# An early load of the query weights' second chunk, and a first unit that gathers partly into the weight ring

## The reference

```python
def peer_ffn(h, wq, sub_keys, u, v):          # wq: 1024 x 2048, u and v: 16384 x 1024
    ...
        q = (xt @ wq).astype(f32).reshape(PEER_TOKEN_BLOCK, PEER_HEADS, 2, PEER_DKEY // 2)
        s = jnp.einsum('thcd,hckd->thck', q, sub_keys.astype(f32))
        top_s, top_i = lax.top_k(s, PEER_TOPK)
        cand = top_s[:, :, 0, :, None] + top_s[:, :, 1, None, :]
        best_s, best_c = lax.top_k(cand.reshape(PEER_TOKEN_BLOCK, PEER_HEADS, PEER_TOPK * PEER_TOPK), PEER_TOPK)
        ...
        expert = i1 * PEER_NKEYS + i2
        w = jax.nn.softmax(best_s, axis=-1)
        act = jax.nn.gelu(jnp.einsum('thkd,td->thk', u[expert].astype(f32), xt.astype(f32)))
        return jnp.einsum('thk,thkd->td', w * act, v[expert].astype(f32))
```

## Time and profile before

| | |
|---|---|
| median of 3 runs | 1526.77 us (1526.72 to 1533.27) |
| the profiled execution: its own time | 1526.57 us |
| its span in the profile | 1524.7 us |
| TensorE busy | 1360.8 us, 89% |
| VectorE busy | 1039.5 us, 68% |
| ScalarE busy | 589.9 us, 39% |
| GpSimd busy | 516.3 us, 34% |
| moved by the DMA engines | 413.69 MB, 271 GB/s over the span |

### The profile page before, as it was taken

How to read it: one execution, slowest core, us unless ns; L and a number is a source line. 1 busy time by engine, 2 the same in 40 slices (tenths; PEclk the granted TensorE clock), 3 DMA queues, 4 the chain that set the end, 5 groups by cost and what they waited for, 6 DMA issues and landing times.

```text
span 1524.7 us, 16289 instructions
## 1 busy us (share of the span) xinstructions
PE 1360.8 (89%) x5950; PEld 900.7 (59%) x5950; DVE 1039.5 (68%) x1860; ACT 589.9 (39%) x908; POOL 516.3 (34%) x554
## 2 busy tenths in 40 slices
PE   9999998777877777777777899999999999999998
PEld 7965677222322222222222368789888897798887
DVE  4655589656666675756557676778897575688963
ACT  4553322212221111111122266855655454555642
POOL 5000046777777777777777600000000000000000
PEclk9999999999999999999999999999999999999999
DMA  9523189999999999999999954326564454356552
GB/s 295 213 78 138 63 334 404 409 409 409 409 409 409 409 409 409 410 409 410 409 409 410 390 180 168 123 97 209 172 216 166 160 201 166 103 174 206 181 195 81
DMA packets 162751, 413.69 MB, mean 271 GB/s; under 512 B 11249, under 2 KB 57579, under 8 KB 162544
## 3 DMA queue, kind: packets, MB, share of 16 engines
q0 software_dynamic: 75664, 272.63, 45.4%
q1 hardware_dynamic: 86832, 139.94, 26.5%
q10 hardware_dynamic: 176, 0.07, 0.0%
HBM read 411.56 MB, written 1.05 MB: 271 GB/s over the span
## 4 chain that ended last, share of the span: by engine, by line
PE 54%; DMA 21%; POOL 8%; DVE 8%; issue 5%; ACT 4%; ACTq 0%; DVEq 0%; POOLq 0%
PE ps L1516 10%; DMA arena<-in_peer_u,routes 9%; PE ps L1536 8%; PE ps L854 7%; PE ps L1352 7%; PE ps L1524 5%; DMA ring<-in_peer_v,routes 5%; POOL arena L3299 4%; DMA aTm<-in_peer_v,routes 3%; DMA proj<-in_peer_v,routes 3%; DVE arena L2826 2%; POOL ring L3310 2%; PE ps L1507 2%; PE ps L1211 1%; PE ps L1239 1%
## 5 line engine op out<-in xcount | busy, mean ns | idle before, releaser
L2826 DVE SCALAR_TENSOR_TENSOR arena<-arena,ps 128x1024 f32<-128x1024 f32 x256 | 312.0, 1219 | 212.8 <-DMA arena<-in_peer_u,routes 211.8
L3299 POOL DMA_INDIRECT arena<-in_peer_u,routes x256 | 249.2, 974 | 113.8 <-DVE arena L2826 50.6
L2054 ACT ACTIVATE state<-cst,gatew 128x128 f32<-128x128 f32 x236 | 88.1, 397 | 307.2 <-PE ps L1352 297.3
L2389 DVE TENSOR_TENSOR w_lo<-ring,w_hi 128x2048 fp32r<-128x2048 f32 x66 | 150.9, 2289 | 71.9 <-ACT w_hi L2201 71.9
L1352 PE MATMUL ps<-ring,state 128*128 128x512 f32 x308 | 150.0, 610 | 45.8 <-ACT state L2054 29.0
L1516 PE MATMUL ps<-x_both,w_hi 128*128 128x512 f32 x640 | 160.3, 392 | 0.0
L2201 ACT ACTIVATE w_hi<-ring 128x2048 fp32r<-128x2048 f32 x66 | 126.0, 1912 | 68.3 <-PE ps L1536 49.9
L1352 PEld LDWEIGHTS ps<-ring,state 128*128 128x128 f32 x308 | 52.5, 189 | 140.5 <-issue 71.5
L1516 PEld LDWEIGHTS ps<-x_both,w_hi 128*128 128x128 f32 x640 | 115.1, 189 | 20.6
L1352 PE MATMUL ps<-proj,state 128*128 128x512 f32 x160 | 78.1, 610 | 24.9 <-ACT state L2054 15.1
L1352 PE MATMUL ps<-wX,state 128*128 128x512 f32 x156 | 76.2, 610 | 23.8 <-ACT state L2054 15.1
(11 more groups left out here) (547 smaller groups left out, 2515.2 us busy)
## 6 DMA issues: line engine op xcount, KB each, us to landing
ring<-in_ffn_w_up SPq DMA_DIRECT2D x22, 2048.0 KB, 8.6
ring<-in_ffn_w_down SPq DMA_DIRECT2D x10, 2048.0 KB, 7.6
ring<-in_even_w_in SPq DMA_DIRECT2D x7, 2048.0 KB, 7.7
ring<-in_w_in SPq DMA_DIRECT2D x6, 2048.0 KB, 10.4
ring<-in_odd_w_in SPq DMA_DIRECT2D x6, 2048.0 KB, 7.7
ring<-in_peer_wq SPq DMA_DIRECT2D x3, 2048.0 KB, 9.4
ring<-in_w_out SPq DMA_DIRECT2D x2, 2048.0 KB, 7.8
arena<-in_peer_u,routes POOLq DMA_INDIRECT x256, 16.0
```

The costliest lines, as they stand in the source:

```text
L2054: do(diags[n % DIAGS], ident, ACT.Copy, scale=gatew[:, u * UROWS + b:u * UROWS + b + 1]).then_inc(diag_ready, 1)
L2389: v.tensor_tensor(w_lo[j % 2][:], w, w_hi[j % 2][:].bitcast(F32), ALU.subtract).then_inc(lo_ready, 1)
L2826: v.scalar_tensor_tensor(row, row, 1.0, token_tile(u // PAIR_UNITS), ALU.mult, ALU.mult, accum_out=dots[:, b:b + 1]).then_inc(u_used, 1)
L3299: pool.indirect_dma_start(arena[:, b % GATHER_SLOTS, :], None, a["peer_u"][0], route_of(u, b))\
```

## The change

The second query chunk, `IN_ARENA`, leaves the ring. It is loaded into the first four places of `arena` as soon as the mixer's recurrent part has read them (`cl_o_done`), ahead of the early pieces of the third chunk, with `consts_in` as its semaphore. Every later chunk of the ring moves up by one place in the order: the fourth query chunk goes where the second was, and follows the first chunk of `w_out`; `ple_gate_w` follows the second chunk of `w_out` and the first query chunk.

Since four places of `arena` hold weights at first, the rows of `peer_u` get new addresses (`u_row`). Places 0 to 3 of the eight are now `arena` 4 to 7. Places 4 to 7 are, for the first 24 rows (`FIRST_ROWS_END`), quarters of the ring place that the second chunk of `w_out` had, and later `arena` 0 to 3. Three waits come with it: the fifth gather waits for the second chunk of `w_out` to be used, the twenty-ninth for the second query chunk, and the load of the first `ple_gate_w` chunk into that ring place for 24 used rows.

```diff
-BESIDE_RING = (CHUNK_AT["peer_wq"] + 2, CHUNK_AT["ple_proj"])
+IN_ARENA = CHUNK_AT["peer_wq"] + 1
+BESIDE_RING = (IN_ARENA, CHUNK_AT["peer_wq"] + 2, CHUNK_AT["ple_proj"])
...
+FIRST_PLACES, FIRST_ROWS_END = RING_PLACE[CHUNK_AT["w_out"] + 1][0], 24
+assert FIRST_PLACES == RING_PLACE[CHUNK_AT["ple_gate_w"]][0]
...
+        def u_row(n):
+
+            at = n % GATHER_SLOTS
+            if at < 4:
+                return arena[:, 4 + at, :]
+            return ring[:, FIRST_PLACES, 1024 * (at - 4):1024 * (at - 3)] if n < FIRST_ROWS_END else arena[:, at - 4, :]
+
         def loaded(i):
 
+            if i == IN_ARENA:
+                return consts_in, 32
             if i in BESIDE_RING:
                 return beside_loaded, 16 * N_BESIDE
...
             n = chunk_width(name, c)
+            if i == IN_ARENA:
+                return grid(block(0, 4), KD, n)
             return slot(i)[:, 0:KD * n].rearrange("p (k n) -> p k n", k=KD)
...
             for i, (name, c) in enumerate(CHUNKS):
-                if i in BESIDE_RING:
+                if i in BESIDE_RING and i != IN_ARENA:
                     continue
...
                     sp.wait_ge(cl_o_done, 2)
+                    sp.dma_start(product_slot(IN_ARENA), weights["peer_wq"][:, :, 512:1024]).then_inc(consts_in, 16)
                     sp.dma_start(grid(query_rows[0], 2, 512), early[:, 0:2, :]).then_inc(beside_loaded, 16)
...
                     sp.dma_start(mixed[:].rearrange("p a (k n) -> p (a k) n", k=2), early[:, 4:8, :]).then_inc(beside_loaded, 16)
+                    continue
                 at, _, _, free = RING_PLACE[i]
                 if free:
                     sp.wait_ge(chunk_done, free)
+                if (name, c) == ("ple_gate_w", 0):
+                    sp.wait_ge(u_used, FIRST_ROWS_END)
...
-                    row = arena[:, b % GATHER_SLOTS, :]
+                    row = u_row(b)
                     dve.wait_ge(u_landed[b % GATHER_SLOTS], 16 * (b // GATHER_SLOTS + 1))
...
-                pool.indirect_dma_start(arena[:, b % GATHER_SLOTS, :], None, a["peer_u"][0], route_of(u, b))\
+                if n == 4:
+                    pool.wait_ge(chunk_done, CHUNK_AT["w_out"] + 2)
+                if n == FIRST_ROWS_END + 4:
+                    pool.wait_ge(chunk_done, IN_ARENA + 1)
+                pool.indirect_dma_start(u_row(n), None, a["peer_u"][0], route_of(u, b))\
                     .then_inc(u_landed[b % GATHER_SLOTS], 16)
```

## The result

The changed kernel takes 1531.22 us (median of 22 runs, 1530.2 to 1532.59), the kernel before 1526.96 us (22 runs, median): a ratio of 1.0026, 95% interval 1.0020 to 1.0032. It is 4.3 us slower; the forecast was 3.8 us. The profiled execution has a span of 1529.1 us, 4.4 more than before.

A forecast was written before the change was run, and what follows sets the result against it. Expert-row gathers at 409 GB/s bound the kernel, VectorE pacing their ramp (201 to 253 us). At 253 us, 3.74 MB gate weights left less 2.17 MB more gathers moved, over 0.409, gives +3.8 us: 1530.4 us; range 1523.5 to 1534.0.

The forecast's parts named there:

- VectorE starts 1.6 us sooner, routes at about 251.3 us: Before the gather plateau: VectorE begins choosing unit 1's experts 1.6 us sooner; routes at 251.3, not 252.92 us.
- Gate loads at 250.0 us: End of the ramp: both ple_gate_w chunks, 4.19 MB, wait for 24 used rows and are issued at 250.0 us.
- Gathers moved by 253 us, 16.25 MB: Ramp, 201 to 253 us: 31 expert rows landed, 16.25 MB, 2.17 MB more than before.
- The estimate of 3.2 us: Ramp: alternative landing time per gathered row, against 4.0 us used; nearly half the thirty-second row in, sum below 0.6 us less.
- 0.45 MB of the gate loads by 253 us: End of the ramp: 0.45 MB of ple_gate_w moved by 253.0 us, 3.74 MB left.
- 308 GB/s between 220 and 250 us: Ramp: gathers alone, paced by VectorE at 1.70 us per 0.524 MB row, move near 308 GB/s in place of 400.
- The plateau starts full: Expert gathers from 253 us on: all bytes left were priced at 0.409 MB/us, with no slower start.
- The first rival: Expert stage from 204 us: DMA engines already full, so 2.1 MB taken out save 5.1 us, 1521.4 us; chance 0.13.
- the start that sets the end: Gather plateau paced by GpSimd's issue, so it ends 1.6 us sooner with the routes: 1525.0 us; chance 0.07.
- The large loss: Ramp: no more than 27 rows in by 253 us, all 4.19 MB gate weights added: 10.2 us, 1536.8 us; chance 0.12.
- The price at nothing of the new addresses and GpSimd's waits: First 32 gathers: their new row places and the added waits of the fifth and twenty-ninth cost nothing.

The follow-up runs named there:

- halved products: VectorE multiplies only 512 of 1024 columns of the first 32 rows: 1524.63 us in the changed kernel, 1526.89 us in the kernel before.
- two extra loads: Changed kernel loading its second gate chunk twice: extra load at about 219 us, 1531.64 and 1531.37 us; both loads after 96 used rows, 1537.03 us.

## Why the prediction was right

The time was right, and so was the mechanism; some terms were off and one was missing, and that they nearly cancel is luck. Term by term:

- *VectorE starts 1.6 us sooner, routes at about 251.3 us*: 1.65 us, and 251.04. TensorE begins on the second query chunk without a wait:

```profile
200.56 7.31 PE L1287 MATMUL ps<-xT,arena 128*128 128x128 f32 x64
```

  But not every gather from the tenth on is issued 1.6 us sooner: the tenth goes out 0.05 us sooner and the eleventh 1.0, at GpSimd's own pace, and only from the thirteenth on it is 1.6. The halved products show that VectorE's instructions are what paces the gathers there.
- *Gate loads at 250.0 us*: 249.99. Their wait alone makes the kernel before 5.8 us slower; that they go out late is the cause of the loss, shown from both kernels.
- *Gathers moved by 253 us, 16.25 MB*: 16.25 MB, but the way there was not clean. I took 4.0 us for a gather to land. None in the ramp did; this is the landing row of the gathers into `arena` up to 253 us in the changed kernel:

```profile
DMA to landing us min/median/max: 5.1/6.0/10.0
```

  So the thirty-first row, issued at 248.44 us, had not landed whole by 253. Bytes of rows under way are moved too, which the step left out; that the two errors cancel to the second decimal is luck. The estimate of 3.2 us that I worked out from the Trainium skill (DMA: Bandwidth & Descriptors, Anatomy of one DMA) lies still further from the 5.1 us at least that were measured; and by that fit 0.7 us of bytes, 0.3 MB of the thirty-second row, would have been in, more than the half that the prediction gave it.
- *0.45 MB of the gate loads by 253 us*: 0.20. With it the sum would have been 1.8 MB and 4.4 us.
- *308 GB/s between 220 and 250 us*: 367, 327 and 311 in the three windows. The rate was reached only at the end, because the first rows, issued at GpSimd's own pace, left a queue that lasted until about 224 us (404 GB/s from 222 to 224 us, 361 in the next two).
- *The plateau starts full*: not so. In the changed kernel 250 to 260 us run at 342 GB/s. The gate loads behind it fill some of this, and without them it is worse by 1.6 us. This term was missing. From 253 to 262 us the changed kernel moves 383 GB/s, the kernel before 407: 0.21 MB, 0.5 us. The tail gave as much back, since from 860 to 875 us the changed kernel moves 409 and the kernel before 395; the prediction had neither.
- The first rival (bytes of a full stage, 5.1 us less) is refuted by the two extra loads; the start that sets the end by the result itself (routes sooner, last row later) and by the halved products. The large loss didn't come either: its condition was 14.1 MB of rows or less by 253 us, and 16.25 were in. The price at nothing of the new addresses and GpSimd's waits stands: with them in place, one load in another order brings the whole loss back.

## What to carry to other kernels

A stage whose transfer engines are full may still have free time in it: ask who would fill it if one of the streams were gone. Here a transfer was nearly free where a compute engine paced the others (0.2 to 0.4 us for 2.1 MB), and cost its bytes divided by the rate or a little more where the engines set the pace (5.3 to 5.8 us); so an early load helps only if what moves up behind it is not pushed out of the free time into the full one. In an in-order queue, look at what the new wait holds back: here a load whose place was free 31 us earlier stood behind one whose place was not.

## What was not expected of the hardware

The DMA share stayed at 0.93 to 0.97 where the changed kernel moved 311 to 367 GB/s, and the same stretch moved 401 to 405 with an extra load in it: a share near one was no sign that the engines could not move more. And a single gather of 0.5 MB took at least 5.1 us to land, median 6.0 us, with no load beside it in most of the ramp, where a plain load of half the size took 3.1 us. The very first gather took 5.1 us too, issued when the engines moved 30 GB/s (201 to 204 us).
